# Two attention heads in half-array products, one normalization on GpSimd, rotary in the projection, modulation groups moved

## Chip, cores and metric

One NeuronCore of a Trainium2 chip runs the whole program in one launch. The metric is the device time of that core in microseconds, the median of several runs. Everything is float32 for the reader of the result; the large products are made of three products of numbers split in a high and a low part.

## What is computed

Two layers over 512 tokens (256 context tokens, 256 latent tokens), width 1024. Each layer has an adaLN-modulated RMSNorm, one input projection, three parallel mixers (attention with a sink, gated linear attention in both directions, a short convolution), an output projection, a gated residual, and then a SwiGLU block, dense in layer 0 and top-2 of 8 experts in layer 1. The modulation vectors of both layers are products of silu(c) with `w_mod` (2 x 1024 x 6144). What the change touches:

```python
def apply_rope(t, cos, sin):
    half = HEAD_DIM // 2
    t1, t2 = t[..., :half], t[..., half:]
    c, s = cos[None, :, None, :], sin[None, :, None, :]
    return jnp.concatenate([t1 * c - t2 * s, t2 * c + t1 * s], axis=-1).astype(t.dtype)

def softmax_with_sink(scores, sink):
    sk = jnp.broadcast_to(sink.astype(F32)[:, :, None, None], scores.shape[:-1] + (1,))
    p = jax.nn.softmax(jnp.concatenate([sk, scores], axis=-1), axis=-1)
    return p[..., 1:]
    # window_attention: latent queries see the context keys and the latent keys within 128 positions
    # context_attention (layer 0 only): context queries see the context keys
```

There are 8 query heads of 64 and 2 key heads. Latent tokens have rotary positions, context tokens don't. In layer 1 only latent queries are needed.

## The kernel before, in words

The order of the work on each engine is written out by hand; each engine runs its own list of instructions and waits on counting semaphores. Stages, with the time of the profile at which they begin: modulation of the first 8 pairs and norm (0), projection 0 (49), linear attention 0 (206), attention 0 (282.9), output projection 0 (370), FFN 0 (about 425), projection 1 (about 797), linear attention 1 (887), attention 1 (951.6), output projection 1 and router (998), experts (about 1060), end at 1518.9.

**Weights** come through a ring of five slots (`raw`, R = 5) that SyncE's DMA queue fills in the order of one list (`stream0`, then FFN, then `stream1`). For a unit of the ring ACT writes its high part (`split_hi`, L503) and DVE its low part (`split_lo`, L508) three units ahead (H = 3) of PE's use. The slot is free after the low part.

**Modulation** is made in 48 pairs, each of two 512 KB units of `w_mod`. `mod_pair` (from L561) waits for both units, and its four products (L576) have two columns of stationary operand each and go to four column groups of PSUM bank 7. After each second pair ACT copies the bank (`mod_rows`, L1052), PE turns it with four transposes (`mod_turns`, L592), and DVE sums it and adds the bias (`mods_in`, L1474 and L1477). Pairs 0 to 7 stand at the start, 8 to 23 in projection 0 (`PROJ_PAIR`: at its units 2 to 22, every fourth left out), 24 to 31 in linear attention 0, one for each of its eight steps, and 32 to 47 in attention 0, one for each second head. Pairs 24 to 47 are those of layer 1. A slot of such a unit is free when PE's pair is done.

**Projection** (`projection`): 16 feature-major units (`fm`, 24 products each), 4 units for v (`tv`) and 4 for the gates (`tg`). The queries are units 12 to 15 (AQ = 12), and in these last units DVE also has the convolution and the first half of the decays (`logits_min`, `log_decay`, `decayed_keys`, `ref_keys`).

**Linear attention** (`gla`): two directions of four steps. A step has the state update (L730, DVE L1657), for tiles with queries the masked product (L743, DVE L1647) and the outputs (L761, L768). At its end PE makes the rotation products of queries and keys (L779), DVE sums up to y (L1683), PE turns y (L789) and ACT and DVE split it.

**Attention** (`attention`): DVE first applies rotary to all queries and keys at once (L1693 to L1704) and writes the keys to `akz`, a copy for each of the two key heads with zeros in the other's 64 rows, so that each score product runs over all 128 rows. Then an item is one head of one tile of 128 queries: 32 items in layer 0 (latent tiles with 4 key blocks, context tiles with 2), 16 in layer 1. PE's order in iteration i: scores(i) (L807) to one of two banks, turn(i-2) (transposes, L817) to one of two banks, in layer 0 a modulation pair, pv(i-3) (L829). DVE: mask (L1739), maximum (L1740), scaling (L1741), and for item i-1 the reciprocal (L1748) and the normalization (L1749). ACT: exp with its row sum (L1238), exp of the sink (L1242), copy of the turned item i-2 (L1249). `prob` has three buffers.

**Output projection** starts in PE's order after the last pv; its first product reads the non-attention tiles first.

## Time and profile before

| | |
|---|---|
| runs | 1526.1, 1529.64, 1532.6 us; median 1529.64 |
| profiled execution | 1520.75 us, its span 1518.9 us |
| busy, share of the span | PE 88%, PE weight loads 72%, DVE 55%, ACT 46%, GpSimd 7% |
| TensorE's granted clock, mean | 0.949 of full speed |
| chain that ended last | PE 78%, DVE 9%, ACT 6%, DMA 4% |
| DMA | 282.78 MB, 186 GB/s over the span |
| issue to landing, 512 KB, median | w_fm 3.6 us; the 18 w_mod loads of the first 40 us 5.1 us |

The profile shows one execution. Busy time of an engine is the time in which one of its instructions ran. L12 is line 12 of the kernel. In a timeline each row has start, duration, engine, line, operation, destination and sources, count (x), and in brackets the idle time before it with what ended it. A float32 product is two records.

### The profile page before, as it was taken

How to read it: one execution, taken by the hardware profiler on the slowest of the kernel's cores; microseconds unless marked ns; L12 is line 12 of the kernel's file. 1: busy time of each engine (PE TensorE's matmuls, PEld its weight loads, DVE VectorE, ACT ScalarE, POOL GpSimd, SP SyncE). 2: the span in 40 equal slices, each digit the busy share in tenths (PEclk: the TensorE clock that was granted, in tenths of full speed). 3: DMA queues.
4: the chain of work that ended last, by engine and by line, in shares of the span. 5: the costliest groups of instructions: out<-in, count | busy, mean ns of one | idle time of the engine just before them, and what ended most of it. 6: DMA issues, size and time to landing. Idle time of an engine off the chain costs nothing.

```text
span 1518.9 us, 21933 instructions
## 1 busy us (share of the span) xinstructions
PE 1343.1 (88%) x7984; PEld 1094.5 (72%) x7984; DVE 841.4 (55%) x1328; ACT 704.4 (46%) x1091; POOL 106.6 (7%) x97
## 2 busy tenths in 40 slices
PE   4799968799989999999989956885999999999993
PEld 0576655356768888888868845583998998899883
DVE  0421286765343333333333486753888988898882
ACT  2622252354352221222334452453777877787771
POOL 4000010000201100111120010020000000000000
PEclk9899989899999999999999977897999999999997
DMA  9364544345222332233212420043799999999992
GB/s 345 117 222 180 183 159 172 110 168 195 97 70 98 114 108 69 85 102 117 99 59 94 146 91 1 1 184 152 262 347 367 371 336 348 368 364 337 361 353 97
DMA packets 74624, 282.78 MB, mean 186 GB/s; under 512 B 8576, under 2 KB 10016, under 8 KB 74432
## 3 DMA queue, kind: packets, MB, share of 16 engines
q1 hardware_dynamic: 68832, 262.17, 48.0%
q0 software_dynamic: 3568, 12.19, 2.2%
q10 hardware_dynamic: 2160, 7.55, 1.3%
q8 instruction: 43, 0.70, 0.2%
q14 instruction: 21, 0.17, 0.0%
HBM read 271.39 MB, written 10.49 MB: 186 GB/s over the span
## 4 chain that ended last, share of the span: by engine, by line
PE 78%; DVE 9%; ACT 6%; DMA 4%; issue 3%; ACTq 0%; POOL 0%; POOLq 0%; SPq 0%; DVEq 0%
PE ps L599 12%; PE ps L601 12%; PE ps L600 12%; PE ps L948 5%; PE ps L950 4%; PE ps L949 4%; PE ps L963 3%; PE ps L967 3%; PE ps L965 3%; PE ps L807 3%; PE ps L576 3%; PE ps L829 3%; DVE wlo L508 2%; ACT whi L503 2%; DMA raw<-in_w_mod 2%
## 5 line engine op out<-in xcount | busy, mean ns | idle before, releaser
L508 DVE TENSOR_TENSOR wlo<-raw,whi 128x1024 fp32r<-128x1024 f32 (+2 forms) x367 | 480.1, 1318 | 329.9 <-ACT whi L503 323.4
L503 ACT ACTIVATE whi<-raw 128x1024 fp32r<-128x1024 f32 (+2 forms) x367 | 410.8, 1125 | 326.9 <-PE ps L601 139.7
L599 PE MATMUL ps<-hhi,whi 128*128 128x512 f32 (+1 forms) x736 | 275.3, 374 | 23.6 <-DVE hlo L1504 21.9
L601 PE MATMUL ps<-hhi,wlo 128*128 128x512 f32 (+1 forms) x736 | 272.3, 370 | 0.0
L600 PE MATMUL ps<-hlo,whi 128*128 128x512 f32 (+1 forms) x736 | 271.1, 368 | 0.0
L948 PE MATMUL ps<-whi,hs_hi 128*128 128x256 f32 x704 | 205.2, 291 | 11.7 <-DVE wlo L508 9.3
L950 PE MATMUL ps<-whi,hs_lo 128*128 128x256 f32 x704 | 197.0, 280 | 0.0
L949 PE MATMUL ps<-wlo,hs_hi 128*128 128x256 f32 x704 | 196.9, 280 | 0.0
L599 PEld LDWEIGHTS ps<-hhi,whi 128*128 128x128 f32 x736 | 139.6, 190 | 58.3 <-issue 32.5
L601 PEld LDWEIGHTS ps<-hhi,wlo 128*128 128x128 f32 x736 | 139.4, 189 | 25.2
L600 PEld LDWEIGHTS ps<-hlo,whi 128*128 128x128 f32 x736 | 139.5, 190 | 24.1
L948 PEld LDWEIGHTS ps<-whi,hs_hi 128*128 128x128 f32 x704 | 133.7, 190 | 14.4 <-DVE wlo L508 10.6
L949 PEld LDWEIGHTS ps<-wlo,hs_hi 128*128 128x128 f32 x704 | 133.8, 190 | 0.4
L950 PEld LDWEIGHTS ps<-whi,hs_lo 128*128 128x128 f32 x704 | 133.4, 190 | 0.0
L963 PE MATMUL ps<-whi,ehi 128*128 128x512 f32 (+3 forms) x224 | 81.2, 362 | 3.7 <-DVE wlo L508 3.7
L965 PE MATMUL ps<-wlo,ehi 128*128 128x512 f32 (+3 forms) x224 | 79.1, 353 | 0.0
L967 PE MATMUL ps<-whi,elo 128*128 128x512 f32 (+3 forms) x224 | 79.1, 353 | 0.0
L576 PE MATMUL ps<-raw,c_act 128*2 128x512 f32 x384 | 56.1, 658 | 21.2 <-DMA raw<-in_w_mod 21.1
L599 PE MATMUL ps<-fhi,whi 128*128 128x512 f32 x176 | 69.3, 394 | 0.0
L601 PE MATMUL ps<-fhi,wlo 128*128 128x512 f32 x176 | 69.0, 392 | 0.0
L600 PE MATMUL ps<-flo,whi 128*128 128x512 f32 x176 | 68.3, 388 | 0.0
L1238 ACT ACTIVATE asc<-ps,negm 128x512 f32<-128x512 f32 (+1 forms) x48 | 29.6, 617 | 65.2 <-DVE negm L1741 65.1
(267 smaller groups left out, 1737.0 us busy)
## 6 DMA issues: line engine op xcount, KB each, us to landing
raw<-in_w_gu SPq DMA_DIRECT2D x230, 512.0 KB, 4.9
raw<-in_w_dn SPq DMA_DIRECT2D x80, 704.0 KB, 8.5
raw<-in_w_mod SPq DMA_DIRECT2D x96, 512.0 KB, 4.5
raw<-in_w_fm SPq DMA_DIRECT2D x32, 512.0 KB, 3.6
raw<-in_w_out SPq DMA_DIRECT2D x16, 512.0 KB, 3.7
raw<-in_w_tg SPq DMA_DIRECT2D x8, 512.0 KB, 3.6
y_rows<-back POOLq DMA_DIRECT2D x1, 4096.0 KB, 18.7
y_rows<-ys ACTq DMA_DIRECT2D x8, 512.0 KB, 6.3
```

What stands on the lines that cost most here:

```text
L503: nc.scalar.activation(whi[:, v % H, 0:cols], src[:, 0:cols], ACT.Copy).then_inc(hi_ready, 1)
L508: nc.vector.tensor_tensor(wlo[:, v % H, 0:cols], landed_in(v)[0][:, 0:cols], whi[:, v % H, 0:cols].bitcast(F32), ALU.subtract).then_inc(lo ...
L576: mm = nc.tensor.matmul(ps[32 * kk:32 * kk + 2, 7, :], c_act[:, 4 * half + kk, :], raw[:, p % R, kk % 2 * 512:kk % 2 * 512 + 512], start=( ...
L599: nc.tensor.matmul(outp, whs, xh, start=first, stop=False)
L600: nc.tensor.matmul(outp, whs, xl, start=False, stop=False)
L601: return nc.tensor.matmul(outp, wls, xh, start=False, stop=last)
L948: nc.tensor.matmul(o, hs_hi[:, k, :], wh, start=(k == 0), stop=False)
L949: nc.tensor.matmul(o, hs_hi[:, k, :], wl, start=False, stop=False)
L950: mm = nc.tensor.matmul(o, hs_lo[:, k, :], wh, start=False, stop=(k == KT - 1))
L963: nc.tensor.matmul(o, ehi[:, j, :], whi[:, s, w:w + n], start=(j == 0), stop=False, skip_group_check=True)
L965: nc.tensor.matmul(o, ehi[:, j, :], wlo[:, s, w:w + n], start=False, stop=False, skip_group_check=True)
L967: mm = nc.tensor.matmul(o, elo[:, j, :], whi[:, s, w:w + n], start=False, stop=(j == FJ - 1), skip_group_check=True)
```

## The change

What it does:

- An attention step is now two heads (kv 0 and 1) of a tile. The scores are two products over 64 rows each, which write two banks; keys are read from `ak` in place and `akz` is gone. The value products of both heads alternate between two column halves. There are two buffers of `prob` (two heads each) and one bank of turned products for each head; before, the turned products had two banks in turn. The copy of step i waits for its own transposes, the transposes of step i for the copies of step i-1.
- Mask, maximum, scaling, sum and reciprocal are one DVE instruction for both heads. The sink term is first added on DVE (`snk`) and then one exp for both. The normalization of head kv 1 is done by GpSimd, that of kv 0 by DVE.
- Rotary is done tile by tile: PE's rotation product for tile n (`turn_pairs`) and three DVE ops (`rope`) in the last units of the projection (keys, first two query tiles) and in the linear attention (the last two), with banks 6 and 7.
- The split of the non-attention tiles (`mixed`) stands inside the first two steps of attention instead of before them.
- Modulation pairs 8 to 23 stand at units 2 to 17 of projection 0, without gaps. Pairs 32 to 47 move from attention 0 to the linear attention of layer 1: none at its first step, four at the second, two at each of the other six. Their loads stand in the ring between the third and fourth unit of output projection 1. The gains for the second norm of layer 1 are made in output projection 1.
- One semaphore instead of two in some places.

```diff
@@ stream
-            if n >= H - 1 and n % 4 != 1 and n_pair < MODT // 2:
+            if n >= H - 1 and n_pair < MODT // 2:
-        stream0 = (pairs(0, START_PAIRS) + proj0 + outs[0][:H] + pairs(PAIR_GLA, MODT) + outs[0][H:])
-        stream1 = PROJ_STAGE[1] + outs[1]
+        stream0 = (pairs(0, START_PAIRS) + proj0 + outs[0][:H] + pairs(PAIR_GLA[0], PAIR_GLA[1]) + outs[0][H:])
+        stream1 = PROJ_STAGE[1] + outs[1][:H] + pairs(PAIR_GLA[1], MODT) + outs[1][H:]
+        def gla_pairs(l, n):
+            first = 0 if l == 0 else 1
+            per = GLA_PAIRS[l] // (2 * NTT)
+            return [] if n < first else range(0 if n == first else n * per, (n + 1) * per)
@@ PE
+            def turn_pairs(l, j):
+                if j >= 2:
+                    pe.wait_ge(rope_ready[l], j - 1)
+                src = aq[:, j - 1, CTX:T] if j else ak[:, CTX:T]
+                nc.tensor.matmul(ps[:, 6 + j % 2, 0:LAT], rot[:, :], src, start=True, stop=True
+                                 ).then_inc(rot_done[l], 1)
...
+                        if n_u == 0:
+                            pe.wait_ge(rope_ready[l], AT + 1)
...
-                    nc.tensor.matmul(ps[:, i % 2, 0:keys(i) * P], aq[:, h // 2, t * P:(t + 1) * P],
-                                     akz[:, h % 2, 0:keys(i) * P], start=True, stop=True).then_inc(s_done[l], 1)
+                        pe.wait_ge(p_ready[l], 2 * (i - 1))
+                    for kv in range(2):
+                        rows = slice(HD * kv, HD * (kv + 1))
+                        nc.tensor.matmul(ps[:, 2 * (i % 2) + kv, 0:keys(t) * P], aq[rows, j, t * P:(t + 1) * P],
+                                         ak[rows, 0:keys(t) * P], start=True, stop=True).then_inc(s_done[l], 1)
...
+                    for kv in range(2):
+                        if kv:
+                            pe.wait_ge(pn2_ready, step0(l) + i + 1)
+                        else:
+                            pe.wait_ge(pn_ready[l], i + 1)
+                        if i:
+                            pe.wait_ge(pT_out[l], 2 * (i - 1) + kv + 1)
...
+                    for k in range(n_k):
+                        for kv in range(2):
+                            mm = nc.tensor.matmul(ps[HD * kv:HD * (kv + 1), 6 + n % 2, j * P:(j + 1) * P],
+                                                  vt[:, k, HD * kv:HD * (kv + 1)],
+                                                  probT[:, i % 2, kv, k * P:(k + 1) * P],
...
@@ ACT
+                        if i >= 2:
+                            act.wait_ge(pT_done[l], 2 * (i - 1))
+                        for kv in range(2):
+                            c = 2 * i + kv
+                            nc.scalar.activation(prob[:, i % 2, kv, 0:keys(t) * P],
...
+                        act.wait_ge(snk_ready, step0(l) + i + 1)
+                        nc.scalar.activation(esink[:, 2 * i:2 * i + 2], snk[:, 2 * i:2 * i + 2], ACT.Exp
+                                             ).then_inc(esk_ready[l], 1)
+                    if 2 <= i < len(todo) + 2:
+                        turned_out(i - 2)
@@ GpSimd
+                    pool.wait_ge(rden_ready, step0(l) + i + 1)
+                    nc.gpsimd.tensor_scalar(prob[:, i % 2, 1, 0:keys(t) * P], prob[:, i % 2, 1, 0:keys(t) * P],
+                                            rden[:, 2 * i + 1:2 * i + 2], None, ALU.mult).then_inc(pn2_ready, 1)
@@ DVE
+            def rope(l, n):
+                dst = aq[:, n - 1, CTX:T] if n else ak[:, CTX:T]
+                turned = rs[:, n % 2 * LAT:(n % 2 + 1) * LAT]
+                dve.wait_ge(rot_done[l], n + 1)
+                V.tensor_tensor(turned, ps[:, 6 + n % 2, 0:LAT], sin[:, :], ALU.mult)
+                then(V.tensor_tensor(dst, dst, cos[:, :], ALU.mult))
+                V.tensor_tensor(dst, dst, turned, ALU.add).then_inc(rope_ready[l], 1)
...
+                        then(V.tensor_reduce(mx[:, c:c + 2], ps[:, b:b + 2, 0:n], AX.X, ALU.max))
...
+                        V.tensor_scalar(prob[:, (i - 1) % 2, 0, 0:n], prob[:, (i - 1) % 2, 0, 0:n],
+                                        rden[:, c - 2:c - 1], None, ALU.mult).then_inc(pn_ready[l], 1)
```

## Rows read from the trace of the kernel before

**Rows 1.** Busy time by stretch: PE, PE loads, DVE, ACT, POOL, clock, DMA share, GB/s.

```profile
54.00:200.00 146.00, 142.12 (x700) 104.10 (x702) 37.81 (x53) 42.38 (x59) 0.00 (x0) 1.00 0.48 177
...
282.85:370.19 87.34, 86.39 (x516) 47.46 (x517) 56.45 (x199) 45.65 (x140) 0.00 (x0) 0.97 0.54 189
...
951.59:997.83 46.24, 43.11 (x224) 26.53 (x224) 32.75 (x101) 23.88 (x65) 0.00 (x0) 0.94 0.00 1
...
897.73:945.66 47.93, 28.15 (x258) 22.98 (x258) 32.38 (x62) 15.08 (x24) 0.00 (x0) 0.70 0.03 11
```

**Rows 2.** Timeline of one steady head in attention 1: start, us, instruction, idle before.

```profile
966.55 1.12 PE L807 MATMUL ps<-akz,aq 128*128 128x512 f32 x2
...
967.51 0.60 PE L817 MATMUL ps<-ident,asc 128*128 128x128 f32 x4
...
967.71 0.30 DVE L1739 TENSOR_TENSOR ps<-ps,amask 128x128 f32<-128x128 f32 x1 [0.45 <-PE ps L807]
...
968.04 1.09 PE L829 MATMUL ps<-asc,vt 128*64 128x128 f32 x8
...
968.05 0.69 DVE L1740 TENSOR_REDUCE mx<-ps 128x1 f32<-128x512 f32 x1
...
968.77 0.21 DVE L1741 TENSOR_SCALAR negm<-mx,negsink 128x1 f32<-128x1 f32 x1
...
969.02 0.69 ACT L1238 ACTIVATE asc<-ps,negm 128x512 f32<-128x512 f32 x1 [1.06 <-DVE negm L1741]
...
969.06 1.12 PE L807 MATMUL ps<-akz,aq 128*128 128x512 f32 x2
...
969.29 0.49 DVE L1749 TENSOR_SCALAR asc<-asc,rden 128x512 f32<-128x512 f32 x1
...
969.70 0.28 ACT L1242 ACTIVATE esink<-sink,negm 128x1 f32<-128x1 f32 x1
...
969.88 0.58 ACT L1249 ACTIVATE asc<-ps 128x512 f32<-128x512 f32 x1
```

**Rows 3.** Timeline, attention 0, a head with two key blocks, ACT.

```profile
343.25 0.47 ACT L1238 ACTIVATE asc<-ps,negm 128x256 f32<-128x256 f32 x1 [0.34 <-DVE negm L1741]
...
343.90 0.37 ACT L1249 ACTIVATE asc<-ps 128x256 f32<-128x256 f32 x1
```

**Rows 4.** Timeline, PE products over part of the rows or columns of the array.

```profile
185.32 1.99 PE L686 MATMUL ps<-la,w 32*128 32x512 f32 x8
...
242.62 0.97 PE L768 MATMUL ps<-state,gqb 128*64 128x64 f32 x16
...
246.68 0.69 PE L730 MATMUL ps<-vt,gkt 128*64 128x64 f32 x16 [2.07 <-ACT gkt L1179]
...
298.71 1.04 PE L576 MATMUL ps<-raw,c_act 128*2 128x512 f32 x8
```

**Rows 5.** Timeline, rotary before attention 1, first and a later op, and the first score.

```profile
945.70 1.23 DVE L1693 TENSOR_TENSOR asc<-aq,cos 128x1024 f32<-128x1024 f32 x1
...
949.81 0.42 DVE L1700 TENSOR_TENSOR asc<-ps,sin 128x256 f32<-128x256 f32 x1
...
951.59 3.78 PE L807 MATMUL ps<-akz,aq 128*128 128x512 f32 x4 [5.21 <-DVE akz L1704]
```

**Rows 6.** Timeline, DVE, start of linear attention 1, the two rows with idle time.

```profile
897.73 1.23 DVE L1586 TENSOR_TENSOR xn<-go,lk 128x1024 f32<-128x1024 f32 x1 [1.07 <-ACT go L1159]
...
902.33 1.39 DVE L1593 SCALAR_TENSOR_TENSOR gqb<-go,lq 64x512 f32<-64x512 f32 x2 [0.51 <-ACT go L1164]
```

**Rows 7.** Timeline, PE, modulation pairs at the start; and the page's issues of w_mod.

```profile
20.75 1.89 PE L576 MATMUL ps<-raw,c_act 128*2 128x512 f32 x8 [2.85 <-DMA raw<-in_w_mod]
...
32.30 1.89 PE L576 MATMUL ps<-raw,c_act 128*2 128x512 f32 x8 [2.08 <-DMA raw<-in_w_mod]
...
raw<-in_w_mod SPq DMA_DIRECT2D x96, 512.0 KB, 4.5
```

**Rows 8.** What the trace has on L1394, GpSimd: duration ns minimum, median, maximum.

```profile
L1394 POOL TENSOR_TENSOR flo<-hf,fhi x22: 1296/1298/1308, 440.4 to 729.5; 128x512 fp32r<-128x512 f32 x22
```

More of the change, by code:

```diff
@@ L371, in cols_of @@
         def cols_of(w):
-            if w < PROJ + OUT:
-                return source(stream0[weights0[w]])[1]
-            if V_PROJ[1] <= w < V_FFN[1]:
-                return source(stream1[w - V_PROJ[1]])[1]
-            return UNIT
+            unit = stream[weights[w]] if w < len(weights) else None
+            return source(unit)[1] if unit and unit[0] not in ("ffn", "expert") else UNIT
         pieces = [[] for _ in range(KT)]
@@ L546, in att_tiles, with steps, keys, step0 @@
             return [2, 3] if l else [2, 3, 0, 1]
+        def steps(l):
+            return [(t, j) for t in att_tiles(l) for j in range(AT)]
+        def keys(t):
+            return 4 if t >= 2 else 2
+        def step0(l):
+            return len(steps(0)) if l else 0
         def gla_tiles(dr):
@@ L774, in gla @@
                         n_o += 1
+                mod_turns((PAIR_GLA[l] + GLA_PAIRS[l]) // 2)
                 pe.wait_ge(o_out[l], n_o)
[L777 to L781 removed]
                 pe.wait_ge(y_ready[l], 1)
[L784 to L785 removed]
+                pe.wait_ge(mod_out, turned[0])
                 pe.wait_ge(st_ready[l], 4 * NTT)
@@ L794, in attention @@
             def attention(l):
-                tiles = att_tiles(l)
-                n_items = len(tiles) * HEADS
-                pe.wait_ge(akz_ready[l], 1)
-                pe.wait_ge(zeroed[l], 2)
-                def keys(i):
-                    return 4 if tiles[i // HEADS] >= 2 else 2
+                todo = steps(l)
+                pe.wait_ge(rope_ready[l], AT + 1)
                 def scores(i):
-                    t, h = tiles[i // HEADS], i % HEADS
+                    t, j = todo[i]
@@ L832, in pv @@
-                    mm.then_inc(pv_done[l], 1)
-                for i in range(n_items + 3):
-                    if i < n_items:
+                    n_k = keys(todo[i][0])
+                    for k in range(n_k):
[3 more added lines that the diff above has]
+                                                  probT[:, i % 2, kv, k * P:(k + 1) * P],
+                                                  start=(k == 0), stop=(k == n_k - 1))
+                            if k == n_k - 1:
+                                mm.then_inc(pv_done[l], 1)
@@ L1217, in attention @@
             def attention(l):
-                tiles = att_tiles(l)
-                n_items = len(tiles) * HEADS
-                def keys(i):
-                    return 4 if tiles[i // HEADS] >= 2 else 2
+                todo = steps(l)
                 def tail(n):
                     act.wait_ge(pv_done[l], HEADS * (n + 1))
-                    t = tiles[n]
+                    t = todo[n * AT][0]
                     nc.scalar.activation(hhi[:, 0:AT, t * P:(t + 1) * P],
-                                         ps[:, 5 + n % 2, :].rearrange("p (j n) -> p j n", j=AT), ACT.Copy
+                                         ps[:, 6 + n % 2, :].rearrange("p (j n) -> p j n", j=AT), ACT.Copy
@@ L1426, in zeros, with attention @@
                 ins.then_inc(zeroed[l], 1)
-                pool.wait_ge(y_ready[l], 1)
-                for n in range(2):
-                    ins = nc.gpsimd.memset(akz[CH * (1 - n):CH * (2 - n), n, :], 0.0)
-                ins.then_inc(zeroed[l], 1)
+            def attention(l):
+                todo = steps(l)
+                for i, (t, j) in enumerate(todo):
+                    pool.wait_ge(rden_ready, step0(l) + i + 1)
+                    nc.gpsimd.tensor_scalar(prob[:, i % 2, 1, 0:keys(t) * P], prob[:, i % 2, 1, 0:keys(t) * P],
+                                            rden[:, 2 * i + 1:2 * i + 2], None, ALU.mult).then_inc(pn2_ready, 1)
             for name, dst in CONSTS(locals_=dict(
@@ L1438, in _ @@
             zeros(0)
+            attention(0)
             norm_add(1)
@@ L1728, in tail @@
                                     ).then_inc(alo_ready[l], 1)
-                for i in range(n_items + 4):
-                    if i >= 11 and i % 8 == 3:
-                        tail((i - 11) // 8)
-                    if i < n_items:
-                        t, h = tiles[i // HEADS], i % HEADS
-                        dve.wait_ge(s_done[l], i + 1)
+                dve.wait_ge(y_ready[l], 1)
+                for i in range(len(todo) + 5):
+                    c = 2 * i
+                    if i < len(todo):
+                        t, j = todo[i]
+                        b, n = 2 * (i % 2), keys(t) * P
+                        dve.wait_ge(s_done[l], 2 * (i + 1))
```

267 lines of the change are left out of this document (120 added, 147 removed).

## The prediction

> **What bounds the kernel now.** I read the page's busy shares first: PE is busy 88% of the span, but as an average over stages with different limits. The table of stretches [rows 1] separates them. In projection 0 PE is busy 142.12 of 146 us: what lengthens PE's work there lengthens the kernel. Both attention stages are nearly as full (86.39 of 87.34 us and 43.11 of 46.24). The linear-attention stage of layer 1, 897.73 to 945.66 (y, the gated sum), has PE busy 28.15 of 47.93 us at a granted clock of 0.70, the level of 2.4 GHz for part of it only: a chain across DVE, ACT and PE sets the time there, and its DMA share is 0.03.
>
> The timeline of a steady head in attention 1 [rows 2] shows why that stage is PE's. PE repeats scores (0.96 us from start to next start), four transposes (0.53), eight value products (1.02): 2.51 us a head. DVE's work for a head fits beside it, with 0.45 us idle, and ACT's too. So I must cost what the change takes from PE, and then look for the loop that comes next.
>
> **Side by side products.** Two heads now go as two row halves (scores) and two column halves (values). The rows nearest [rows 4]: the modulation product puts four column groups next to each other, eight records of 512 columns in 1.04 us, where two such records of one full product take 1.12 [rows 2]; so column groups run together. The state update alternates two column halves, 16 records in 0.69 us, against 0.97 for 16 records of the same size that stay in one half. For row groups only L686 is there (32 rows): four products of 512 columns in 1.99 us, where four full ones take about 3.8. I take scores of two heads 0.96, values 1.02, transposes 2 x 0.53 = 1.06: 3.04 us instead of 5.02. Bounds for scores and values: half of that again (L686 per product), or no overlap, 5.02.
>
> A rule speaks against this: the Trainium skill, TensorEngine Tiling (Array Packing), section Key Properties, says that changing the tiling mode drains TensorE, and a step has three modes (row halves, full, column halves). In [rows 2] each change between full and half width shows a gap of at most 0.17 us; by the rule one more such gap a step, 24 x 0.17 = 4 us, an estimate, would be added if PE were the limit.
>
> **The loop that comes next.** In the new order PE issues scores(i), turn(i-2), pv(i-3). ACT issues two exps, one sink exp, then the two copies of turned step i-2. The turned products now have one bank for each half, so turn(i-1) waits for copy(i-2) and this stands behind exp(i). From scores(i): product 1.16 to DVE's start; DVE mask 0.34 + 0.13 for 128 columns more, maximum over 1024 columns instead of 512, 0.72 + 0.55, scaling to ACT's start 0.25: 1.99 (the additions by some 1.05 ns a column, an estimate from 0.69 for 512 columns with its fixed part taken off). ACT: two exps at 0.68, sink to copy 0.18, two copies about 0.6 each: 2.74 [rows 2]. Then PE: 0.04, second turn 0.53, values 1.02, and scores(i+2) may go. The sum is 7.5 us for two steps, **3.74 us a step** of two heads instead of 5.02. The shorter loop from the second copy through turn(i-1) and exp(i+1) to the next second copy is 3.5; DVE's own work about 3.0; PE's 3.04. So ACT's order, not PE, bounds it, and half of PE's gain is given back; the mode gaps above have cover of 0.7 us a step. On the two context tiles (two key blocks instead of four) the shorter loop is the longer of the two: half the turn 0.28, to the next exp 0.17, two exps at 0.46, sink 0.19, two copies 0.39 each: 2.36 a step [rows 3].
>
> The normalization of the second head on GpSimd has no row. The nearest is a two-input op on 128x512, 1.30 us [rows 8]; one input can cost less, I bound it by 0.5 (DVE's, [rows 2]) and 2.2. The reciprocal is ready 3.64 after scores(i) starts and the turn of that half starts at 5.9, so up to 2.2 us is hidden: nothing.
>
> Attention 1: both orders start cold. The first exps wait for the split of the mix (four DVE ops) and for a chain without overlap: exp(2) starts 10.1 after the first score, then 5 steps of 3.74 to exp(7), 28.8; from there exps, normalization, turn, copy, values of the last steps 7.5: 36.3 against 46.24, **-9.9 us**. Attention 0: exp(2) at 11.0, six steps of 3.74, seven of 2.36 to exp(15) at about 49.7, 5 for the end: 54.7. Before, 87.34, of which 16 modulation pairs (17.48 us of PE work and the gaps around it) are gone from here: **-32.6 us**.
>
> **Rotary.** It leaves the stretch between the last sum of the linear part and the first score: 945.70 to 951.6 on DVE, with PE waiting 5.21 us for akz [rows 5]; 5.9 us a layer, 11.8 in all. The zeroing of akz on GpSimd goes too and costs nothing (beside it). It comes back as five groups of three DVE ops on 256 columns, 0.35 + 0.46 + 0.35 = 1.16 us each [rows 5] (by L1700), 5.8 a layer, three of them in the last units of the projection and two between the query products. DVE has just two holes there, 1.07 and 0.51 us [rows 6]; the rest is on the chain. The rotation products on PE (0.43 us a record of 512 columns [rows 2], half for 256) now lie in the projection's end and before the turned keys, where ACT and DVE are later than PE: free. u(0) also waits for the last rotary group, as DVE does. Net per layer: +5.8 - 1.1 (hole) - 5.9, in layer 1 a hole more: -1.1 and **-1.5 us**.
>
> **Modulation groups.** In projection 0 the 16 pairs stand at units 2 to 17 in a row instead of with gaps. One pair more (1.04 + half a turn 0.25) comes before the unit at which DVE's chain takes over, and the v units are shorter than the time from a pair's end to a split weight (landing 3.6 in the table above, split on ACT and DVE 1.1 + 1.2), 0.8 us each at four units, where PE lost 3.9 us in all before [rows 1]: **+2 us** (0 to +4).
>
> The 16 pairs of layer 1 move from attention 0, where their 1 MB each came in under cover, to the linear stage of layer 1, four at its second step and two at each of the six after. Each pair is 1.04 us of PE and 0.27 of turns, 21 us against 19.8 us that PE is idle there; DVE and ACT get 16 small ops. But the loads bound it: the ring of five slots is full when the stage begins, so 2.5 pairs are there, and 13.5 must be fetched. At the start of the kernel, where only loads bound, pairs followed each other at 2.9 us (four intervals between 20.75 and 32.30 [rows 7]). Followed step by step with 4.5 us to landing [rows 7]: first pair at 907.6, the three last pairs of step 1 end at 918, the first direction ends at 934 instead of 921.7, the last pair at 958, the last sum (before 945.66) at 964.3, first score at 965.1 instead of 951.59: +13.5, of which rotary is -1.5, so the pairs cost **+15 us**. Bounds: +6 if their work only filled PE's idle and raised its clock (a pair takes 1.89 us at the lower clock [rows 7], 1.04 at the higher [rows 4]), +22 if pairs come at 3.5.
>
> Small: the last turn and gains of layer 1 leave out-projection 0 (-0.4) and a gain comes to out-projection 1 (+0.2). DMA streams after it, FFN and experts are untouched.
>
> **Sum:** -9.9 - 32.6 - 1.1 - 1.5 + 2 + 15 - 0.2 = **-28.3 us**. The profiled execution took 1520.75 (span 1518.9 and 1.9 around it), so it becomes 1492.4. It lies 8.9 under the median of the runs, 1529.64; against that median the forecast is **1501 us**.
>
> **Rivals.** (A) Halves don't overlap (the change doesn't do what its name says). A step is 5.0 and 2.9 us: attention 0 saves only the pairs, about -17, attention 1 +2, the rest as above +14: 1529. Against it: the column rows [rows 4]; for it: no row with 64-row halves. Only the row halves failing gives +0.43 us a step by the loop, at most 10 us in 24 steps: 1510.
>
> (B) The ring serializes (slower). If a step's pairs wait for each other's loads, since PE holds a pair in order before it frees slots, a pair costs landing and use, 5.1 (the table above, loads at the start) + 1.04 = 6.1 us, and 14 of them 85 us from 907.6: the last sum comes at 993, 29 us later than forecast: 1530 with all the rest as forecast; with PE clocked down in these waits, as the pairs of [rows 7] were, 0.85 us more for a pair's products and as much for each step's own, eight times: 1538. It decides from 5.0 us a pair. For it: PE's in-order wait holds am and state behind it. Against: 2.9 at the start with the same ring.
>
> (C) GpSimd is the bound. Its op and DVE's could take turns at the data: if it waits for DVE's scaling, 0.49 us [rows 2], and takes 2.2 itself, it ends 0.5 after its cover, 12 us over 24 steps: 1513. Against it: 1.30 for an op with two inputs, with DVE at work beside it [rows 8]. The Trainium skill, SBUF: State Buffer, section SBUF: two separate sides, gives such a rule: DVE in a 2-port mode and GpSimd exclude each other for a whole instruction. DVE's one-input op took 0.49 where its maximum over as many columns took 0.69, so that mode may be at work; by the rule alone, without the 2.2, the wait stays under cover.
>
> (D) PE's gaps make the clock fall to 1.2 GHz in attention. PE's part doubles in the loop, +1.5 us a step: 1537. Against it: gaps would be 0.7 us, and in linear stage 0 PE was idle 2.07 us ahead of L730's 16 records, which still took 0.69 [rows 4].
>
> **Chances.** Forecast with its own bounds (1490 to 1512) 0.78; A or its half 0.09; B 0.05; C 0.05; D 0.03. A measurement of this kernel tells about 0.5% (7.6 us) from no change. Faster by more: the forecast, C and half of A, 0.88; within: 0.07; slower: 0.05 (D and the worse half of B). The range 1487 to 1516 takes in C and partial overlap.
>
> **What would show it.** Timeline of attention 1: scores to scores 3.7 us, PE waiting for ACT's copy before the second turn; if instead it waits for GpSimd, C. The scores of both heads within 1.1 us, else A. Linear stage 1: DMA share above 0.8, PE waiting for w_mod, y at 19 us later relative to the projection's end; pairs 2.9 apart. Attention 0 about 55 us long. Rotary ops 1.2 us a group on DVE without a hole. Wrong would be: a step longer than 4.4 us, pairs more than 3.5 us apart, or a stage that isn't touched changing by more than 2 us.

## The result, and the profile after

The kernel after takes 1516.5 us (median of five runs, 1514.6 to 1518.5) where the kernel before took 1526.9 beside it: a ratio of 0.9925, 95% interval 0.9902 to 0.9947. The forecast was 1501; the change gave 10.4 us and not 28, and the time lies just outside the range of 1487 to 1516. The profiled executions differ by less, 1520.75 and 1515.81 us, since that of before lies below all the timed runs of that kernel beside it. In what follows sums of stages compare profiled executions, and verdicts compare medians.

Start with the stretches of the kernel after that answer to [rows 1]: projection 0, attention 0 from its first score to the out-projection, part of linear attention 1, attention 1.

```profile
54.00:200.00 146.00, 139.72 (x682) 99.75 (x681) 36.39 (x52) 37.27 (x52) 0.00 (x0) 1.00 0.53 187
285.44:347.77 62.33, 47.71 (x353) 28.42 (x353) 38.47 (x111) 37.41 (x119) 23.46 (x16) 0.86 0.00 1
...
895.00:948.00 53.00, 38.70 (x367) 19.32 (x360) 24.95 (x63) 12.42 (x20) 0.00 (x0) 0.94 0.81 290
...
954.45:991.00 36.55, 29.00 (x193) 16.48 (x192) 23.57 (x61) 21.68 (x60) 14.85 (x8) 0.79 0.01 1
```

Attention 0 went from 87.34 to 62.33 us, and PE is busy 77% of it, no longer 99%: another engine's order sets the time. Its DMA share went from 0.54 to 0.00 and that of linear attention 1 from 0.03 to 0.81; that is the move of the modulation weights. Attention 1 went from 46.24 to 38.6 us (954.45 to 993.05), the way from the end of FFN 0 to the first score of layer 1 from 158.9 to 176.2.

The granted clock fell in both attentions, from 0.97 to 0.86 and from 0.94 to 0.79. Both kernels start them at the lower level (0.50, which is 1.2 GHz). The kernel before leaves it after 5 to 6 us and stays at 1.00. The kernel after is at the lower level for 12 of the first 19 us of attention 0, where the clock rises for 3 us and falls again after PE was all but idle from 288 to 291, and for 15 of the first 17 us of attention 1. Here are 289 to 301 of before, then of after, with most of the start of attention 1 and a piece of the part of attention 0 that has two key blocks a step ("two-key" below, against "four-key"):

```profile
289.00:301.00 12.00, 11.05 (x69) 6.16 (x68) 7.86 (x26) 6.14 (x17) 0.00 (x0) 1.00 0.52 181
```

```profile
289.00:301.00 12.00, 7.58 (x24) 3.76 (x24) 9.64 (x23) 5.60 (x17) 3.71 (x2) 0.57 0.00 0
...
955.00:969.00 14.00, 10.66 (x30) 4.36 (x27) 10.02 (x24) 6.53 (x20) 3.71 (x2) 0.50 0.00 1
...
335.00:340.00 5.00, 4.69 (x30) 2.66 (x28) 2.19 (x8) 3.10 (x14) 2.03 (x2) 0.68 0.01 2
```

In these 12 us PE was idle for 4.4 us in the kernel after and for 1 us in the kernel before, which had two modulation pairs there.

A steady step of two heads in attention 1 of the kernel after, to be read against [rows 2]:

```profile
972.36 1.23 DVE L1760 TENSOR_REDUCE mx<-ps 128x2 f32<-128x1024 f32 x1
...
973.05 1.09 PE L851 MATMUL ps<-probT,vt 128*64 128x128 f32 x16
...
974.07 1.13 PE L824 MATMUL ps<-ak,aq 64*128 64x512 f32 x4
...
974.28 0.49 DVE L1776 TENSOR_SCALAR prob<-prob,rden 128x512 f32<-128x512 f32 x1
...
974.34 1.86 POOL L1454 TENSOR_SCALAR prob<-prob,rden 128x512 f32<-128x512 f32 x1 [2.43 <-DVE rden L1774]
...
975.25 1.08 ACT L1253 ACTIVATE probT<-ps 128x512 f32<-128x512 f32 x2
...
975.74 1.22 DVE L1760 TENSOR_REDUCE mx<-ps 128x2 f32<-128x1024 f32 x1
...
975.98 1.12 PE L838 MATMUL ps<-ident,prob 128*128 128x128 f32 x8 [0.78 <-ACT probT L1253]
```

Both heads' scores take 1.13 us where one head's took 1.12, both heads' values 1.09 for 16 records where eight took 1.09: the halves of the array do run side by side. A step is 3.4 and 4.0 us in turn (maximum to maximum 972.36, 975.74, 979.72), 3.7 on average, the forecast's 3.74, and PE waits for ScalarE's copy, as forecast. GpSimd's operation takes 1.86 us, inside the bounds of 0.5 and 2.2, and PE waits here for the copy, not for it.

GpSimd's 1.86 us may not be all its own work. It starts 0.06 us after VectorE's scaling nearly every time, and VectorE is then busy with that for 0.43 us more. Where it started later in VectorE's operation it was shorter by as much. In e11, a kernel of the next section:

```profile
969.51 0.69 DVE L1776 TENSOR_SCALAR prob<-prob,rden 128x512 f32<-128x512 f32 x1
...
969.91 1.72 POOL L1454 TENSOR_SCALAR prob<-prob,rden 128x512 f32<-128x512 f32 x1
```

Time less overlap is 1.43 us where it takes 1.86 and 1.42 where it takes 1.72; with two key blocks it is 0.79 us both for 1.08 and for 1.03 us. So the operation looks as if it waited for VectorE's, as rival C had it. No kernel here runs the one without the other, so that is a reading of eleven odd cases in thirteen traces and not a test.

What the forecast did not have on its list is a stage that the change doesn't touch. FFN 0, from the table load of one norm to that of the next, went from 374.1 to 380.8 us. Stretch 600 to 700 of the kernel before run again, then of the kernel after:

```profile
600.00:700.00 100.00, 100.00 (x439) 82.05 (x438) 30.96 (x30) 27.13 (x34) 10.39 (x8) 1.00 0.28 92
```

```profile
600.00:700.00 100.00, 100.00 (x430) 80.60 (x429) 31.68 (x28) 29.42 (x38) 11.72 (x9) 1.00 0.30 104
```

PE is 100% busy in both, at full clock, with the same matmuls of 512 columns: 439 in 100 us before, 430 after. From start to start they come every 0.2289 us before and every 0.2333 us after, and so in the projections too; 374.1 us by the ratio of these two would be 381.3. A busy share can't show that; a count in a fixed window does.

### The profile page after: what moved, and what is told of

It reads as the page before. It is cut to its first block, busy times and chain, and to the rows that moved or that the text cites. A ratio compares the mean times of both kernels' runs of the same rounds, so it can differ in the third digit from the quotient of the medians.

```text
span 1514.0 us, 21813 instructions
## 1 busy us (share of the span) xinstructions
PE 1322.6 (87%) x7984; PEld 1072.5 (71%) x7984; DVE 815.7 (54%) x1228; ACT 696.5 (46%) x1067; POOL 142.9 (9%) x117
## 4 chain that ended last, share of the span: by engine, by line
PE 73%; DVE 9%; ACT 7%; DMA 6%; issue 3%; POOL 1%; ACTq 0%; POOLq 0%; SPq 0%; DVEq 0%
PE ps L603 12%; PE ps L604 12%; PE ps L605 12%; PE ps L968 5%; PE ps L970 4%; PE ps L969 4%; DMA raw<-in_w_mod 3%; PE ps L983 3%; PE ps L987 3%; PE ps L985 3%; PE ps L580 3%; DVE wlo L497 2%; ACT whi L492 2%; PE ps L675 1%; PE ps L838 1%
## 5 line engine op out<-in xcount | busy, mean ns | idle before, releaser
L604 PE MATMUL ps<-hlo,whi 128*128 128x512 f32 (+1 forms) x736 | 274.6, 373 | 0.0
L1300 ACT ACTIVATE fhi<-hf 128x512 fp32r<-128x512 f32 x22 | 13.9, 632 | 98.7 <-DVE hf L1810 98.7
```

What stands on the lines that cost most here:

```text
L604: nc.tensor.matmul(outp, whs, xl, start=False, stop=False)
```

## The experiments

Every ratio below is to the kernel before on the same chip, with its 95% interval. The kernel before took 1525.8 us beside e1 to e8 and 1524.7 and 1524.6 us beside e9 to e12 and e13 to e16, so that times of different groups can be set side by side to about 1 us, apart from their own spread. "The layout of before" is explained by the first group.

### Why the same matmuls became slower

The change adds one small tensor, `snk`, 128 bytes a partition, ahead of the split activations `hhi`, `hlo`, `fhi`, `flo`, which PE streams. Four kernels ran together.

e1_before: no edit.

> The kernel before, unchanged, as the measure of noise and of the pitch of the 512-column matmuls of the FFN on this chip. Both theories: ratio 1.00 (0.998 to 1.002). Memory layout theory: pitch 0.2283 us again, as in the profile of before (from 599.70 to 603.82). Chip or execution theory (the pitch differs from one chip or execution to another): 0.2283 or 0.2333, and the same in all four kernels of this call.

e2_before_pad, on the kernel before:

```diff
+        pad = sb("pad", [P, NTT * HEADS])
         esink = sb("esink", [P, NTT * HEADS])
```

> The kernel before with one more tensor of 128 bytes a partition, never written, in front of the tensor esink: nothing else is changed, and what lies behind it moves by the 128 bytes by which the changed kernel moves it. Layout theory: the FFN's matmuls come every 0.2333 us as after the change, the FFN of each layer is 8 us longer (374 to 382), and with the projections the kernel is 10 to 17 us slower than before, ratio 1.007 to 1.011. Chip or execution theory, and code theory (the pitch comes with the changed instructions): ratio 1.00, pitch as in the kernel before.

e3_after_snk, on the kernel after:

```diff
-        snk = sb("snk", [P, NTT * HEADS])
...
         pick = sb("pick", [P, 2, 2, NE])
+        snk = pick[:, :, :, :].rearrange("p a b e -> p (a b e)")
```

> The kernel after with its new 128-byte tensor (the difference of sink and maximum) laid over another small tensor that is not in use at that time, so that all that lies behind it is where it was before the change. Layout theory: pitch 0.2283 us, some 8 us less in each FFN that showed 382 us, 10 to 17 us in all: 1500 to 1506 us, ratio to before 0.980 to 0.986. Chip, execution and code theories: as the kernel after, ratio 0.9925.

e4_after: the kernel after, no edit.

> The kernel after, unchanged, on the chip of the other three. Layout and code theories: ratio 0.9925 (0.990 to 0.995) and pitch 0.2333 us. Chip or execution theory: the pitch of this run is that of the kernel before in the same call; if that is one pitch for both, the ratio should come to about 0.985, which is 10 us less than measured, so this theory needs the first measurement to have been an accident of chips.

Measured: e1 1525.6 us, ratio 1.0007 (0.9989 to 1.0025). e2 1534.5 us, 1.0048 (1.0033 to 1.0062): slower beyond doubt, but by 8.7 us, less than the 10 to 17 expected (1.007 to 1.011). e3 1505.35 us, 0.9853 (0.9833 to 0.9873). e4 1517.5 us, 0.9938 (0.9920 to 0.9957). The stretch 600 to 700 of e2 and then of e3:

```profile
600.00:700.00 100.00, 100.00 (x430) 80.17 (x429) 29.89 (x30) 25.07 (x31) 9.03 (x7) 1.00 0.27 86
```

```profile
600.00:700.00 100.00, 100.00 (x439) 82.05 (x438) 31.78 (x28) 30.00 (x38) 12.99 (x10) 1.00 0.33 110
```

An unused tensor of 128 bytes makes the kernel before as slow in FFN 0 as the kernel after; laying `snk` over a tensor that isn't in use gives the kernel after its 374.4 us back. Theories of the chip, of the execution and of the code fall: between e3 and e4 lie 12.2 us, and the edit changes nothing but places in memory.

What about the place? Four more kernels.

e5_pad256, on the kernel after:

```diff
         snk = sb("snk", [P, NTT * HEADS])
+        pad = sb("pad", [P, NTT * HEADS])
```

> The kernel after with another 128-byte tensor, never written, beside its new one: what lies behind is moved by 256 bytes against before, not 128. Alignment theory (the pitch of the 512-column matmuls hangs on where the streamed operand lies within 256 bytes): 0.2289 us again and about 1505 us, ratio 0.985. Distance theory (it hangs on having kept the exact addresses of before): 0.2333 us and 1516 to 1518 us, ratio 0.993.

e9_mod0 and e10_mod128, on e3_after_snk, with 16 and with 48 floats:

```diff
+        pad = sb("pad", [P, 16])
         esink = sb("esink", [P, NTT * HEADS])
```

> The kernel after with the layout of before, and 64 bytes more in front of the streamed operands. The addresses of the compiled kernels say that they start at 192 in 256 bytes in the kernels with the 0.2289 us pitch and at 64 in those with 0.2333 us; here at 0. Theory that the pitch is two-valued (a half of the 256 bytes): one of the two pitches. Theory that it grows with the distance to a boundary: a third value, below 0.2289 us, towards 0.22; the FFN of layer 0 then takes 365 to 370 us, not 374.

> The same with 192 bytes more: the streamed operands start at 128 in 256 bytes, as the stationary ones (whi, wlo) do. Two-valued theory: one of the two pitches. Theory that the stationary and the streamed operand disturb each other where they lie alike: the slowest pitch, 0.2333 us or more. Theory of the distance to a boundary: between 0.2289 and 0.2333 us.

e15_stat, on the kernel after:

```diff
+        pad = sb("pad", [P, 32])
         whi = sb("whi", [P, H, DUNIT], F32R)
```

> The kernel after with the stationary operands (whi, wlo) moved by 128 bytes to 0 in 256 and the streamed ones at 192 as in before. Theory that only the streamed operand's place counts: pitch 0.2289 us in projections and FFN. Theory that the distance between stationary and streamed operand counts (192 less 0 is the distance of the kernel after, 64 less 128): 0.2333 us. In the experts, where the roles are the other way round, the first theory lets the time change and the second too.

Measured, with the addresses modulo 256 (the traces don't show them; how far two tensors lie apart follows from the sizes declared in each kernel between them). "Pitch" is the time from the start of one matmul to the start of the next, over some 130 of FFN 0; "streamed" is the place of `hhi`, `hlo`, `fhi`, `flo`, "stationary" that of `whi` and `wlo`, the operand that is loaded into the array:

| kernel | streamed | stationary | difference | pitch, us | time, us |
|---|---|---|---|---|---|
| before, e1, e3 | 192 | 128 | 64 | 0.2289 | 1505.35 (e3) |
| e5_pad256 | 192 | 128 | 64 | 0.2289 | 1506.0 |
| after, e2, e4 | 64 | 128 | 192 | 0.2333 | 1517.5 (e4) |
| e9_mod0 | 0 | 128 | 128 | 0.2333 | 1522.9, one run |
| e15_stat | 192 | 0 | 192 | 0.2333 | 1513.8, one run |
| e10_mod128 | 128 | 128 | 0 | 0.2267 | 1505.8, one run |

e5's ratio is 0.9868 (0.9832 to 0.9903). The rows of e10 and of e15:

```profile
600.00:700.00 100.00, 100.00 (x443) 82.79 (x442) 31.82 (x28) 29.43 (x37) 11.72 (x9) 1.00 0.34 112
```

```profile
600.00:700.00 100.00, 100.00 (x430) 80.60 (x429) 31.68 (x28) 28.48 (x37) 11.71 (x9) 1.00 0.32 108
```

The streamed operand's place alone is not it: 192 goes with 0.2289 in one row and, with the stationary operand moved, with 0.2333 in e15. The difference of the two fits all rows: fastest at 0, then 64, slow at 128 and 192. These are five different pairs of places, and one kernel, e15, tells the difference from the streamed place alone; that is a rule that fits, not a proven one, and no run shows why. The theory on record that operands which lie alike disturb each other gave e10 the slowest pitch; it has the fastest. In e10 FFN 0 is 3.5 us shorter than in e3 (370.9), but the stretch from the last norm to the end is 498.1 and not 495.0 us: the experts' operands had moved too.

The experts show that "alike is best" is no rule. There the roles are changed, `whi` and `wlo` are streamed in 256 columns against `hs_hi` and `hs_lo`. In stretches of 20 and more such matmuls in a row the pitch is 0.1154 us in e3, 0.1178 in both e4 and e15, 0.1191 in e9 and 0.1198 in e10. Streamed less stationary is 192, 64, 64, 128 and 0 there: again one pitch for each difference, but now 192 is the fastest and 0 the slowest.

### Where the modulation pairs stand

e6_gla168, on e3_after_snk:

```diff
-        START_PAIRS, GLA_PAIRS = M0 // 2, [8, 16]
+        START_PAIRS, GLA_PAIRS = M0 // 2, [16, 8]
```

> The kernel after with the layout of before, and with 16 modulation pairs in the linear attention of layer 0 and 8 in that of layer 1, not 8 and 16. Theory of my forecast (a pair costs 0.94 us wherever TensorE takes it): linear attention 1 becomes 7.5 us shorter and linear attention 0 7.5 us longer, ratio as the kernel after with the layout of before, 0.985. Rival (in layer 1 the pairs wait for their weights, which come in 5.6 to 6.2 us a pair after another, while in layer 0 they have landed): layer 1 gains 12 us and layer 0 loses 4 to 8, ratio 0.980 to 0.983.

Measured: 1496.7 us, 0.9797 (0.9766 to 0.9828), 8.7 us less than e3. In the profiled executions the first score of layer 0 comes 10.2 us later (285.84 to 296.00), and the way from FFN 0's end to the first score of layer 1 falls from 173.4 to 155.6 us. So eight pairs more cost 1.3 us each in layer 0, and eight fewer give back 2.2 each in layer 1. The rival's mechanism holds; both sizes are above those it gave (4 to 8 and 12 us). PE's waits for the modulation weights in linear attention 1 (in total, times, longest), of the kernel after (895 to 945 us) and of e6 (880 to 936 us):

```profile
PE ps L580 <- DMA raw<-in_w_mod: 12.2, 7, 2.7
```

```profile
PE ps L580 <- DMA raw<-in_w_mod: 0.4, 1, 0.4
```

and two of the four places in the kernel after's chain of waits where a load is the path (start, us):

```profile
897.87 6.22 DMA raw<-in_w_mod
...
911.09 6.06 DMA raw<-in_w_mod
```

With eight pairs there the loads are in time and only PE's own 1.04 us a pair is left; that it fills holes is read from the 155.6 us, 3.3 less than the kernel before takes with no pairs there.

### The loop in attention

Four kernels, all on e3_after_snk, change who waits for whom. For each I read the starts of the maximum (L1760 in e3) and what PE waits for.

e7_dve_norm takes the second head's normalization from GpSimd to VectorE:

```diff
                         V.tensor_scalar(prob[:, (i - 1) % 2, 0, 0:n], ..., ALU.mult).then_inc(pn_ready[l], 1)
+                        V.tensor_scalar(prob[:, (i - 1) % 2, 1, 0:n], prob[:, (i - 1) % 2, 1, 0:n],
+                                        rden[:, c - 1:c], None, ALU.mult).then_inc(pn2_ready, 1)
```

> The kernel after with the layout of before, and the second head's normalization on VectorE like the first head's, GpSimd doing none. GpSimd-under-cover theory (my forecast): the steps with four key blocks stay at 3.7 us, and so do those with two: 0 to +3 us for 0.49 us more of VectorE a step. Rival, GpSimd in the two-step loop where there are two key blocks only (2.85 us a step measured, 2.36 forecast): its 1.08 us becomes 0.35 us, the eight steps of two key blocks come to 2.4 to 2.5 us and the kernel is 3 to 4 us faster, ratio 0.983. Rival, GpSimd on the path throughout: 24 steps by 0.5 us or more, 12 us faster, ratio 0.977.

Measured: 1504.3 us, 0.9871 (0.9826 to 0.9916), 1 us less than e3 and not to be told from it. The steps of four key blocks are 3.74 and 3.62 us in turn, on average as in e3; those of two go from 2.85 to 2.67 on average, half of what the rival gave. So GpSimd is under cover in the steady four-key steps of this order. Elsewhere the traces show a little more than the medians: from the first score to the out-projection attention 0 takes 60.01 us for 62.30 in e3, and attention 1, which has no two-key steps, 36.85 for 38.75. The four times of e7 lie between 1500.1 and 1512.9 us, too far apart to settle 4 us.

e8_act_order puts ScalarE's copies first:

```diff
                 for i in range(len(todo) + 5):
+                    if 2 <= i < len(todo) + 2:
+                        turned_out(i - 2)
                     if i < len(todo):
...
-                    if 2 <= i < len(todo) + 2:
-                        turned_out(i - 2)
```

> The kernel after with the layout of before, and ScalarE taking the copies of step i-2 ahead of the exponentials of step i, not behind them. Theory of my forecast (a four-key step is the loop exponentials, copies, second head's turn, next exponentials, since one bank for a head holds the turned block): the loop opens and the 16 steps of four key blocks fall from 3.7 to 3.1 to 3.5 us, the kernel is 3 to 9 us faster, ratio 0.979 to 0.983. Rival (the path is VectorE to GpSimd to turns, whatever ScalarE's order): no change or slower, ratio 0.985 to 0.988, as the copies now hold the exponentials back until the turn is done.

Measured: 1501.65 us, 0.9827 (0.9793 to 0.9860), 3.7 less; the intervals of e8 and e3 overlap, so what follows rests on the traces. The four-key steps are 3.6 us and not 3.7, the two-key steps 2.5 and not 2.85. PE's waits in attention 0, of e3 and then of e8:

```profile
PE ps L838 <- ACT probT L1253: 7.1, 11, 1.8
...
PE ps L838 <- POOL prob L1454: 0.3, 1, 0.3
```

```profile
PE ps L838 <- POOL prob L1454: 3.4, 8, 0.8
```

The wait for the copies is gone, and one for GpSimd stands in its place. My theory of the loop was right, my 3.1 to 3.5 us was not: the next loop begins 0.1 us below. Attention 0 is 58.53 us long, attention 1 37.12.

e11_tail: VectorE takes the low part of a finished tile a step later.

```diff
-                    if i >= AT + 3 and (i - 3) % AT == 0:
-                        tail((i - 3) // AT - 1)
+                    if i >= AT + 4 and (i - 4) % AT == 0:
+                        tail((i - 4) // AT - 1)
```

> The kernel after with the layout of before, and VectorE taking the low part of a finished tile one step later, so that it no longer waits 1.4 us for ScalarE's high part ahead of the next step's normalization. Theory (that wait is what makes every other step of two key blocks 3.7 us long): the eight steps fall from 2.85 to about 2.5 us and the kernel is 2 to 4 us faster, ratio 0.983 to 0.984. Rival (the step waits for GpSimd and the turns anyway): same as without, ratio 0.985 to 0.987.

Measured: 1504.2 us, 0.9888 (0.9850 to 0.9927): by the times of the runs it can't be told from e3. The traces do tell. VectorE in e3, then in e11:

```profile
319.97 0.69 DVE L1743 TENSOR_TENSOR hlo<-ps,hhi 128x512 fp32r<-128x512 f32 x1 [2.08 <-ACT hhi L1243]
...
332.16 0.69 DVE L1743 TENSOR_TENSOR hlo<-ps,hhi 128x512 fp32r<-128x512 f32 x1 [1.36 <-ACT hhi L1243]
```

```profile
321.45 0.68 DVE L1743 TENSOR_TENSOR hlo<-ps,hhi 128x512 fp32r<-128x512 f32 x1
...
332.29 0.68 DVE L1743 TENSOR_TENSOR hlo<-ps,hhi 128x512 fp32r<-128x512 f32 x1
```

VectorE stood 2.1 and 1.4 us in front of the finished tiles, with the next normalization queued behind. Without that the stretch from the first maximum to the last falls from 51.99 to 48.35 us, and the change from four key blocks to two from 5.10 to 3.09. A part of this is the clock: in e3 it falls in the two-key part (0.72 from 334 to 340 us) and at the end, in e11 it stays at 1.00 there (334 to 339 and 340.4 to 343.4).

e14_serial gives up the alternation of the value products:

```diff
-                    for k in range(n_k):
-                        for kv in range(2):
+                    for kv in range(2):
+                        for k in range(n_k):
```

> The kernel after with the layout of before, and the value products of the first head issued all ahead of those of the second, not alternating: what they compute is the same. Theory of my forecast (the column halves of the array run side by side only where their products alternate, and TensorE is near the path): 1.09 us for 16 products becomes 1.9 to 2.1 us, 24 steps, of which a part is hidden: 5 to 15 us slower, ratio 0.989 to 0.995. Rival (the halves overlap in any order, or TensorE's time is hidden): ratio 0.985 to 0.987.

Measured: 1513.1 us, 0.9924 (0.9904 to 0.9943), 7.8 us slower than e3. One step's values in e14 (1.09 us in e3):

```profile
306.61 1.58 PE L851 MATMUL ps<-probT,vt 128*64 128x128 f32 x16
```

Alternation is worth 0.49 us a step, less than my 0.8 to 1.0, so the halves overlap in part in any order. Between the profiled executions lie 5.6 us, and in the two attentions I find only 1.6 of them (52.96 and 26.70 us between the first and last maximum for 51.99 and 26.12). Of the rest, 1.7 us in layer 0 and 1.5 in layer 1 lie ahead of the attentions, where there are no value products. The first score of layer 0 stands anywhere from 285.3 to 287.5 us in the traces of e3, e5, e7, e8, e11 and e14, which are alike up to there, so this part need not come from the edit. The median fell in the range given, but in the traces the attentions carry only 1.6 to 2.6 of the 5.6 us.

### All of it together

e12_both is e8 with e6's edit. e13_best adds e11's and puts both groups of streamed operands where they ran best:

```diff
+        pad = sb("pad", [P, 48])
         esink = sb("esink", [P, NTT * HEADS])
...
+        pad2 = sb("pad2", [P, 16], F32, region)
         htm = sb("htm", [P, 2, D], F32, region)
```

e16_best_dve is e13 with e7's edit.

> The kernel after with the layout of before, 16 modulation pairs in the linear attention of layer 0 and 8 in layer 1, and the copies ahead of the exponentials on ScalarE. If the two gains add (9 us and 3 to 4 us alone): 1492 to 1494 us, ratio 0.977 to 0.978. If the attention's gain comes from where the pairs left a hole: 1496 us, ratio 0.980.

> All that gained, in one kernel: the modulation pairs 16 and 8, ScalarE's copies ahead of the exponentials, VectorE's low part of a finished tile one step later, the streamed operands of projections and FFN at 128 in 256 bytes and those of the experts left at 192. By the traces: 1493 us for the first two, 3.6 us less in attention 0 for the third, 3.5 us less in FFN 0 and 1 to 2 us in the projections for the fourth: 1484 to 1487 us, ratio 0.973 to 0.975. Rival (the third opens the same hole as ScalarE's order): 1487 to 1490 us.

> As the kernel with all that gained, and the second head's normalization on VectorE too. Theory that GpSimd's 1.86 and 1.08 us are still in the two-step loop once the other stalls are gone: 2 to 6 us faster than with GpSimd, 1480 to 1484 us. Rival (ScalarE is the path then, and VectorE's 0.49 us a step comes on top): 0 to 4 us slower than with GpSimd.

Measured: e12 1493.3 us, 0.9810 (0.9770 to 0.9851); e13 1483.9 us, 0.9724 (0.9703 to 0.9746); e16 1474.4 us, 0.9668 (0.9649 to 0.9687), some 40 us below the kernel after. e12 can't be told from e6 (3.4 us less, the intervals overlap); e13 and e16 are each clear of what they build on. Taking GpSimd out gives 9.6 us here by the medians, where e7 gave 1 that could as well have been 5. The traces make the contrast smaller: the two attentions together are 4.2 us shorter in e7 than in e3, and 7.2 in e16 than in e13 (54.03 to 50.23 and 36.28 to 32.92). The 2 to 6 us expected were too little. What PE still waits for at GpSimd in attention 0 of e13, then one step of VectorE in e16, from mask to mask (the rows left out follow each other too):

```profile
PE ps L840 <- POOL prob L1456: 2.9, 6, 0.8
```

```profile
311.88 0.43 DVE L1751 TENSOR_TENSOR ps<-ps,amask 128x256 f32<-128x256 f32 x1
...
312.34 1.23 DVE L1753 TENSOR_REDUCE mx<-ps 128x2 f32<-128x1024 f32 x1
...
315.06 0.43 DVE L1751 TENSOR_TENSOR ps<-ps,amask 128x256 f32<-128x256 f32 x1
```

A four-key step is 3.18 us there, the same each time, and VectorE has no idle time in it: it is the bound of these steps now.

## Why the prediction was wrong, step by step

**The steady loop: right.** 3.74 us forecast, 3.7 measured, and e8 shows ScalarE's order to be what sets it. The halves overlap (1.13 and 1.09 us for two heads, as long as for one before), so rival A falls.

**Rival D, the clock: wrong in the loop, right around it.** In the steady four-key steps the clock is at its higher level (1.00 from 303 to 316 us in e3). But the starts run at 0.50 for 6 to 10 us longer than in the kernel before, and in attention 0 of e3 one step's scores take 2.08 us there for 1.13; in its two-key part one step's turn, values and scores take 1.11, 1.06 and 1.23 us for 0.68, 0.66 and 0.70, and at the end 16 value records take 1.98 for 1.09. These differences add up to 3.2 us of attention 0, an estimate that holds if all of them lay on the path. The forecast had PE's gaps as free; D had their price only as 1.5 us on every step.

**"FFN and experts are untouched": wrong, and the largest miss.** The step that failed is the list of what the change touches. It reads the instructions and not the addresses, and `snk` moved every streamed operand by 128 bytes. Worth 12.2 us by e3 against e4; of this 0.0044 us on each of some 2200 matmuls is 9.7 us. The experts' pitch changed too (0.1154 to 0.1178 us), but their stretch is only 0.8 us longer. With the layout undone the forecast's 1501 stands against 1505.35, inside its range. That is in part luck: the gain is then 20.4 us and not 28.3, and the number comes close because the kernel before took 1525.8 us beside e3 and not the 1529.64 that the forecast starts from. My own line for being wrong, an untouched stage that changes by over 2 us, is the one that struck.

**Attention 0: mis-sized, the second miss.** -32.6 forecast, -25.0 measured. In e3 it takes 62.30 us where I had 54.7. Part by part, forecast in brackets: first score to exp(2) 12.3 us (11.0), six steps to exp(8) 23.3 (22.4), seven two-key steps to exp(15) 20.0 (16.5), from there to the out-projection 6.7 (5). My own parts add up to 54.9, not 54.7. The largest is the two-key part, and the step into it took 5.10 us from maximum to maximum. I had followed the loop through ScalarE and left out VectorE's queue: the finished tile's low part (e11) and GpSimd's 1.08 us (e7, half of it) are what is late there, and the clock falls with them. The start and the end ran at the lower clock for the most part; how much of their excess is the clock no run parts. Attention 1 lacks the two-key part and came out nearer: 38.6 us, forecast 36.3; its five steady steps took 18.9 us for 18.7, its start and its end about 1 us more each.

**Modulation pairs: right in sum, wrong in kind.** The first score of layer 1 moved by 17.3 us in the kernel after and 14.5 in e3 with the old pitch, +13.5 forecast. But it is not a price for each pair: e6 gets 17.8 us back for eight pairs, and with eight left the stretch is 155.6 us, under the 158.9 of before. Rival B's mechanism, pairs that wait in order for their loads, was at work four times at about 6 us; the other loads came under cover. The 16 pairs started 3.4 us apart on average (894.2 to 945.5), just under my sign for being wrong, 3.5, and not the 2.9 of the kernel's start. Projection 0's +2 was right: its end, the first op of the log decay, moved from 205.18 to 207.58 in e3. From there to the first score it took 78.3 us for 77.7 before, +0.6 where the rotary was to give -1.1: mis-sized by 1.7, and no run parts it further.

**GpSimd: right here, by little cover.** 1.86 us, bounds 0.5 to 2.2, hidden in the steady steps of the kernel after. Rival C's wait for VectorE's scaling seems to be in these 1.86 us, its price is not: it needed 2.2 us and the wait on top. e8, e13 and e16 show how near it was: open any other loop and it is on the path.

**The sum by profiled executions.** Before to e3, that is without the layout: +3.0 to the first score of layer 0 against +0.9 forecast, -24.4 from there to the norm against -32.6, FFN 0 +0.3 against 0, +14.5 against +13.5, attention and out-projection 1 -7.5 against -9.9, the rest +0.1 against -0.2. That is -13.9 us against -28.3. The medians of e3 and of before lie 20.4 apart, so some 6 us of the gain depend on which execution is read. By the traces the parts other than the layout thus gave half of what was forecast, most of the lack in attention 0.

## What to carry to other kernels

A new tensor moves all that is allocated behind it: where a kernel streams from fixed places, count the matmuls of a fully busy stretch before and after, and try the layout before blaming the change. In a loop of several engines, work out the second and third longest loop too: a gain of one edit ends where the next loop begins (3.74 to 3.6 us here), and an edit that can't be told from nothing alone can be worth 7 to 10 us with the others. A stage with less work for PE can also stay at the lower clock for longer (12 and 15 us here for 5 and 6): look at the granted clock of its first microseconds. Loads that are moved into a stage with few other loads cost nothing up to what the ring brings in, and then their whole landing time.

## What the runs showed of the hardware

PE's pitch for back-to-back products of 512 columns, with weights loaded for each, changed with the places of the two operands: 0.2267 us where streamed and stationary operand start alike modulo 256 bytes, 0.2289 with 64 bytes between them, 0.2333 with 128 and 192. For the experts' products of 256 columns the order is another one: 0.1154 with 192, 0.1178 with 64, 0.1191 with 128, 0.1198 where they start alike. The Trainium skill, TensorE: Matmul & The Clock Gate, section Wait — 56ns, not 53.3ns?, gives 215.7 ns for 512 columns at the higher clock; no layout tried here reached it.

Two heads' products over row halves or alternating column halves of the array took as long as one head's (1.13 and 1.09 us). With all of one column half issued first the values took 1.58 us.

GpSimd takes 1.86 us to scale 128x512 by one number a row and 1.08 for 128x256, where VectorE needs 0.49 and 0.35; about 0.43 and 0.29 us of that look like waiting for VectorE's operation. Even without it, 1.43 us, that is more than its addition of two such tensors in [rows 8], against my guess that one input costs less.
